# Vectors loaded as rows and turned by TensorE, an output product begun one channel early, a softmax maximum in one reduction

## The reference, cut to what matters

```python
# attention, projection (context 256 tokens, then 1024 tokens)
h = rms_norm(x, norm_w) * (1 + scale) + shift        # shift, scale, norm_w: vectors of 1024
q_a, k_a, v_a, c_q, c_kv, k_pe, gate = split(h @ w_in)
q_a = rms_norm(q_a, q_norm_w); k_a = rms_norm(k_a, k_norm_w)    # per head of 64
c_q, c_kv = rms_norm(c_q, cq_w), rms_norm(c_kv, ckv_w)
# attention, 16 heads, 1280 keys
p = softmax(q @ k.T * scale); o = p @ v
# hyena, projection: a convolution of 3 taps with a bias per channel, 3072 channels
u = sum(pad(h @ w_in)[:, j:j + L] * conv_w[j] for j in range(3)) + conv_b
# even mixer, projection: a causal convolution of 31 taps over 512 channels, with a bias
u = causal_dwconv(a_val * sigmoid(a_gate), dw_w, dw_b)
# recurrence: h_t = a_t h_(t-1) + b_t over the tokens, for 1024 channels, then
y = (gelu(y_branch) * h) @ out_w
```

## Time and profile before

| | |
|---|---|
| median of 3 runs | 5271.82 us (5264.84 to 5273.2) |
| profiled execution, its own time | 5277.84 us |
| its span | 5276.1 us |
| PE busy | 4409.4 us, 84% of the span |
| DVE, ACT, GpSimd busy | 1938.4 us, 1097.2 us, 276.5 us |

### The profile page before, as it was taken

The page is one execution under the profiler, slowest core; times in us unless marked ns, Lnnn a source line. Parts: engine busy times, 40 slices in busy tenths (PEclk is TensorE's granted clock), DMA queues, the critical chain, the costliest instruction groups (busy, mean ns, idle before and its releaser), DMA issues. The chain is left out here.

```text
span 5276.1 us, 52830 instructions
## 1 busy us (share of the span) xinstructions
PE 4409.4 (84%) x18126; PEld 2298.7 (44%) x18126; DVE 1938.4 (37%) x3064; ACT 1097.2 (21%) x1726; POOL 276.5 (5%) x390
## 2 busy tenths in 40 slices
PE   2599688997699988999689977869998598879995
PEld 0355455554344435777344445443332243533332
DVE  1233455443212205988439465321111333321112
ACT  0122344442111102222020344000000243100001
POOL 0000000000000000111000000000001000000001
PEclk7799899998899998999899988879999699789998
DMA  6322221113444411111330112356644420366655
GB/s 240 109 63 66 57 48 35 34 34 120 146 170 178 172 43 64 50 50 49 128 116 32 47 70 80 129 243 261 245 170 151 144 72 24 117 244 235 269 186 199
DMA packets 284026, 644.83 MB, mean 122 GB/s; under 512 B 92357, under 2 KB 172117, under 8 KB 264449
## 3 DMA queue, kind: packets, MB, share of 16 engines
q1 hardware_dynamic: 247594, 514.27, 28.2%
q0 software_dynamic: 21856, 102.40, 5.0%
q10 hardware_dynamic: 14456, 26.58, 1.3%
HBM read 915.53 MB, written 117.73 MB: 196 GB/s over the span
## 5 line engine op out<-in xcount | busy, mean ns | idle before, releaser
L3325 PE MATMUL blocks_h<-moe_w,blocks_xT 128*64 128x512 f32 x3072 | 694.0, 605 | 21.4 <-issue 15.3
L3325 PEld LDWEIGHTS blocks_h<-moe_w,blocks_xT 128*64 128x64 f32 x3072 | 223.6, 139 | 447.6 <-issue 442.6
L1630 PE MATMUL hyp_acc<-hy_hT,hyp_weights 128*128 128x512 f32 x768 | 337.7, 599 | 40.2 <-DMA hyp_weights<-in_hy_w_in 40.2
L3346 PE MATMUL blocks_acc<-moe_w,blocks_hidT 128*64 128x512 f32 x1536 | 340.1, 595 | 1.6 <-DVE blocks_hidT L3238 1.6
L1069 PE MATMUL att_scores<-att_kT,att_qT 64*128 64x512 f32 (+3 forms) x768 | 251.3, 546 | 21.2 <-DMA att_v<-scratch_V 21.2
L799 PE MATMUL lat_acc<-lat_w_in,lat_hT 128*128 128x512 f32 (+1 forms) x640 | 244.8, 538 | 1.5 <-DVE lat_hT L683 1.5
L1630 PEld LDWEIGHTS hyp_acc<-hy_hT,hyp_weights 128*128 128x128 f32 x768 | 146.3, 193 | 217.0 <-issue 217.0
L1093 PE MATMUL att_turn<-ident,att_probs 128*128 128x128 f32 x1280 | 192.2, 281 | 56.3 <-ACT att_probsT L981 32.1
L2166 PE MATMUL evp_acc<-ev_hT,evp_weights 128*128 128x512 f32 x512 | 225.5, 602 | 7.6 <-DVE evp_qkT L2307 5.6
L1004 DVE TENSOR_REDUCE att_parts<-att_scores 128x1 f32<-128x1024 f32 (+1 forms) x256 | 198.7, 818 | 73.5 <-PE att_scores L1069 73.5
L970 ACT ACTIVATE att_probs<-att_scores,att_nmax 128x1280 f32<-128x1280 f32 x128 | 170.0, 1328 | 193.5 <-DVE att_nmax L1006 193.5
(11 more groups left out here) (476 smaller groups left out, 5910.4 us busy)
## 6 DMA issues: line engine op xcount, KB each, us to landing
moe_w<-in_ex_w SPq DMA_DIRECT2D x288, 2048.0 KB
hyp_m_weights<-in_mod_w POOLq DMA_DIRECT2D x6, 8192.0 KB, 24.1
mod_weights<-in_ada_w SPq DMA_DIRECT2D x6, 4096.0 KB, 23.2
scratch_y_rows<-blocks_y ACTq DMA_DIRECT2D x48, 512.0 KB, 8.3
hyp_weights<-in_hy_w_in SPq DMA_DIRECT2D x8, 2048.0 KB, 27.4
scratch_parts<-hyp_uT SPq DMA_DIRECT2D x24, 512.0 KB, 3.5
evp_weights<-in_ev_in_w SPq DMA_DIRECT2D x5, 2048.0 KB, 12.7
lat_w_in<-in_attn_w_in SPq DMA_DIRECT2D x4, 2048.0 KB, 18.0
```

What stands on the lines that cost most here:

```text
L1630: mm = nc.tensor.matmul(acc[:, m % 2, half * NC:(half + 1) * NC], weights[:, ws, kt, c:c + P], hT[:, kt, half * NC:(half + 1) * NC], start ...
L3325: mm = nc.tensor.matmul(out[mine, :], xT[:, s, kt, mine], w[:, l, kt, :], start=(kt == 0), stop=(kt == KT - 1))
L3346: mm = nc.tensor.matmul(acc[mine, c, :], hidT[:, kt, mine], w2[:, l, kt, c * NC:(c + 1) * NC], start=(kt == 0), stop=(kt == FT - 1))
```

## The change

Five places change.

1. In the attention projection (both runs) the three vectors are loaded as 24 rows of 128 into `col_rows` and turned by one PE transpose; DVE copies them to `cols`. SP loads x of tile 0, the rows, the first chunk of `w_in`, x of tile 1, then the rest. The four loads of head norm weights move from SP's to ScalarE's queue, under a semaphore of their own, and DVE waits for them after the first tile's `hT`. ACT squares before it waits for `gain`.
2. In attention one reduction over 1280 columns takes the place of two reductions and the minimum.
3. In the hyena projection taps and bias are loaded as 96 rows of 128, turned by one PE transpose and copied by DVE.
4. In the even projection the tap rows come first in SP's queue; the bias moves behind the second weights, with a semaphore that DVE alone waits for.
5. In the recurrence the first two token tiles use px and py, and their products over channel tiles 0 to 6 begin when tile 6 is scanned; the last matmul of each follows when tile 7 is.

```diff
@@ attention_project, SP
-                for s in range(S):
-                    load_x(0, s)
+                load_x(0, 0)
                 for n, v in enumerate((d["mods"][vec, 0:D], d["mods"][vec, D:2 * D], d["norm_w"][0])):
-                    sp.dma_start(cols[:, n, :], columns(v), allow_slow_non_contiguous=True).then_inc(cols_in, 16)
-                for dst, v, count in ((w_head[:, 0:GQ, :], "attn_q_norm", GQ), (w_head[:, GQ:, :], "attn_k_norm", GKV)):
...
-                sp.dma_start(w_low[:, 0:MQR], row(d["mla_q_norm"][0], P)).then_inc(cols_in, 16)
-                sp.dma_start(w_low[:, MQR:], row(d["mla_kv_norm"][0], P)).then_inc(cols_in, 16)
+                    sp.dma_start(col_rows[n * KT:(n + 1) * KT, :], v.rearrange("(kt p) -> kt p", p=P)).then_inc(cols_in, 16)
                 for c, (a, b) in enumerate(chunks):
                     sp.dma_start(w_in[:, :, a:b], wv[:, :, a:b]).then_inc(w_chunk_in[c], 16)
+                    if c == 0:
+                        load_x(0, 1)
@@ ACT
-                act.wait_ge(prepared, signals(1))
+                for dst, v, count in ((w_head[:, 0:GQ, :], "attn_q_norm", GQ), (w_head[:, GQ:, :], "attn_k_norm", GKV)):
+                    act.dma_start(dst, row(d[v][0], P).unsqueeze(1).to_broadcast([P, count, HD])).then_inc(heads_in, 16)
+                act.dma_start(w_low[:, 0:MQR], row(d["mla_q_norm"][0], P)).then_inc(heads_in, 16)
+                act.dma_start(w_low[:, MQR:], row(d["mla_kv_norm"][0], P)).then_inc(heads_in, 16)
...
                 def prepare(n, s):
                     square(n, s)
+                    act.wait_ge(prepared, signals(1))
                     modulate(n, s)
@@ DVE
-                dve.wait_ge(cols_in, signals(16 * 7))
...
+                def columns_ready():
+                    dve.wait_ge(cols_turned, signals(1))
+                    nc.vector.tensor_copy(cols[:, :, :].rearrange("p v kt -> p (v kt)"), up[:, 0, 0:3 * KT]).then_inc(cols_ready, 1)
+                    dve.wait_ge(cols_ready, signals(1))
...
+                def head_weights_ready():
+                    dve.wait_ge(heads_in, signals(16 * 4))
...
                 def prepare(n, s):
+                    columns_ready()
                     norm(n, s)
                     modulate(n, s)
+                    head_weights_ready()
@@ PE
+                pe.wait_ge(cols_in, signals(16 * 3))
+                nc.tensor.transpose(up[:, 0, 0:3 * KT], col_rows[:, :], ident[0:3 * KT, 0:3 * KT]).then_inc(cols_turned, 1)
                 pe.sem_inc(copied, 2)
@@ stage_attention, DVE maximum
-                    b = j % 2
-                    for i, (ready, a, z) in enumerate(((front_scored, 0, 2 * NC), (scored, 2 * NC, KEYS))):
-                        dve.wait_ge(ready, signals(n * PAIR + (j + 1)))
-                        nc.vector.tensor_reduce(parts[:, b, i:i + 1], scores[:, b, a:z], AX.X, ALU.max, negate=True).then_inc(halved, 1)
-                    dve.wait_ge(halved, signals(n * (2 * PAIR) + (2 * j + 2)))
-                    nc.vector.tensor_tensor(nmax[:, b:b + 1], parts[:, b, 0:1], parts[:, b, 1:2], ALU.min).then_inc(maxed, 1)
+                    dve.wait_ge(scored, signals(n * PAIR + (j + 1)))
+                    nc.vector.tensor_reduce(nmax[:, j % 2:j % 2 + 1], scores[:, j % 2, 0:KEYS], AX.X, ALU.max,
+                                            negate=True).then_inc(maxed, 1)
@@ stage_hyena_project
-                for j in range(TAPS):
-                    sp.dma_start(taps[:, j, :], columns(d["hy_conv_w"][0, j]), allow_slow_non_contiguous=True)\
-                        .then_inc(taps_in, 16)
-                sp.dma_start(bias[:, :], columns(d["hy_conv_b"][0]), allow_slow_non_contiguous=True).then_inc(taps_in, 16)
+                sp.dma_start(tap_rows[0:TAPS * COLS, :], d["hy_conv_w"][0].rearrange("j (q p) -> (j q) p", p=P)).then_inc(taps_in, 16)
+                sp.dma_start(tap_rows[TAPS * COLS:, :], d["hy_conv_b"].rearrange("a (q p) -> (a q) p", p=P)).then_inc(taps_in, 16)
@@ PE, ahead of pe.sem_inc(product, CH_TILES)
+                pe.wait_ge(taps_in, signals(32))
+                rows = (TAPS + 1) * COLS
+                nc.tensor.transpose(turn[:, 0, 0, 0:rows], tap_rows[:, :], ident[0:rows, 0:rows]).then_inc(taps_turned, 1)
@@ stage_even_project, SP
+                sp.dma_start(tap_rows[:, :], d["ev_dw_w_2"][0]).then_inc(taps_in, 16)
                 load(1, 1)
-                sp.dma_start(tap_rows[:, :], d["ev_dw_w_2"][0]).then_inc(taps_in, 16)
-                sp.dma_start(bias[:, :], columns(d["ev_dw_b_2"][0]), allow_slow_non_contiguous=True).then_inc(taps_in, 16)
                 load(0, 0)
+                sp.dma_start(bias[:, :], columns(d["ev_dw_b_2"][0]), allow_slow_non_contiguous=True).then_inc(bias_in, 16)
@@ PE
-                pe.wait_ge(taps_in, signals(32))
+                pe.wait_ge(taps_in, signals(16))
@@ stage_recurrence, PE
+                pe.wait_ge(scanned, signals(KT - 1))
+                pe.wait_ge(conved, signals(KT))
+                pe.wait_ge(gelued, signals(KT))
+                for t in range(2):
+                    for c in range(2):
+                        output(t, c, range(KT - 1))
                 pe.wait_ge(scanned, signals(KT))
...
+                for t in range(2):
                     for c in range(2):
...
+                        output(t, c, [KT - 1]).then_inc(product, 1)
+                for t in range(2, TT):
+                    for c in range(2):
+                        pe.wait_ge(scaled, signals(2 * t + c - 3))
+                        output(t, c, range(KT)).then_inc(product, 1)
```

More of the change, by code:

```diff
@@ L1475, in stage_hyena_project @@
         weights = sb("weights", [P, 2, KT, NC])
-        taps, bias = sb("taps", [P, TAPS, HY_PARTS * CH_TILES]), sb("bias", [P, HY_PARTS * CH_TILES])
+        COLS = HY_PARTS * CH_TILES
+        tap_rows, taps = sb("tap_rows", [(TAPS + 1) * COLS, P]), sb("taps", [P, TAPS + 1, COLS])
         u = sb("u", [P, 2, L])
@@ L1487, in stage_hyena_project @@
         w_in = [sem(f"w_in{s}") for s in range(2)]
[L1488 to L1489 removed]
+        taps_in, taps_turned, taps_ready, product, centred, sides, conved, turned, uT_act, uT_dve = (
+            sem(n) for n in ("taps_in", "taps_turned", "taps_ready", "product", "centred", "sides", "conved", "turned", "uT_act", "uT_dve"))
         part_out = [sem(f"part_out{s}") for s in range(2)]
@@ L1564, in centre @@
                     act.wait_ge(turned, signals(q * 2))
-                    nc.scalar.activation(u[:, s, :], acc[:, s, :], ACT.Identity, bias=bias[:, bass.ds(q, 1)],
+                    nc.scalar.activation(u[:, s, :], acc[:, s, :], ACT.Identity, bias=taps[:, TAPS, bass.ds(q, 1)],
                                          scale=taps[:, 1, bass.ds(q, 1)]).then_inc(centred, 1)
```

48 lines of the change are left out of this document (25 added, 23 removed).

## The result

The changed kernel takes **5225.6 us** (median of 4 runs, 5223.0 to 5229.7) against 5270.5 (4 runs of the kernel before beside it): ratio 0.9917, 95% interval 0.9900 to 0.9934. Forecast were 5200.7 us and a range of 5184 to 5225. The profiled execution has a span of 5224.6 us against 5276.1. The sign was right, the size was not: 71.1 us were forecast, 51.5 came between the spans and 45 between the medians. The profiled execution of the kernel before was itself 7.4 us slower than its median, the one of the changed kernel 0.8, so some 6 us of what the two traces differ by need not be the change's.

What follows compares the result with a forecast made beforehand. PE, busy 84% of the span, was taken to lose time in idle stretches waiting for loads and other engines. Gains 36 + 13 + 8.4 + 2 + 11.7 = 71.1 us gave 5200.7 us, range 5184 to 5225.

Steps and rivals of the forecast that it cites:

- Part 1: Attention projection, `ctx` and `lat`: earlier first products gain 18 us each, 36 in all, ends 32.9 and 43.9.
- If they alternate one for one and the repeated reads keep their own pace of 83 per us: Attention projection: `w_in`'s first chunk beside head weights takes 13.8 us, product starts at 108, gain 16.3 us in `ctx`.
- the turned columns hide in it: Attention projection: transposing and copying 24 row pieces fits within the 6.64 us from ACT's square to first product.
- Rival (a): Attention projection: head weights still hold SP's queue up; two stages give 12 us, not 36; 5224.7 us; chance 0.17.
- Rival (b): Attention projection: the queues do not hinder each other at all; 43.9 us instead of 36; 5192.8 us; chance 0.20.
- Part 2: Attention's softmax maximum: one reduction shortens 57 waits by 0.24 us each; gain 13 us, ends 0 and 18.
- (c): Attention gains nothing because the later maximum takes the wait's place; 13 us less, 5213.7 us; chance 0.10.
- (d): Attention slower: exponent due once each tile is scored, longer tail loses 117 us; 5331 us; chance 0.03.
- Part 3: Hyena projection: 96 pieces of 512 B replace 12,288 of 4 bytes; gain 8.4 us, ends 6.5 and 14.
- Part 4: Even projection: transposes stop waiting for the bias, gate weights then decide; gain 2 us, ends 1 and 3.2.
- Rival (e): Hyena and even projections gain nothing, weights still waiting for other traffic; 10.4 us less, 5211 us; chance 0.06.
- Part 5: Recurrence's end: output products start after tile 6 is scanned; gain 11.7 us, ends 10.5 and 12.5.

Runs made afterwards that it cites:

- 8 heads after x: Changed kernel, but ScalarE issues the repeated head weights only once x has landed, some 4 us later; 5219.8 us (0.9892).
- 5 columns on ScalarE: Changed kernel with the three column-row loads moved from SP's to ScalarE's queue, ahead of the head weights; 5209.0 us (0.9880).
- 6 one load ahead: Changed kernel with two of three column-row loads on ScalarE's queue, only the norm weight's rows left ahead of `w_in`; 5218.1 us (0.9900).
- 7 w_in first: Changed kernel with the three column-row loads put behind `w_in`'s first chunk in SP's queue; 5236.9 us (0.9932).
- 6 columns merged: Changed kernel with shift and scale rows in one load instead of two; 5225.7 us (0.9912).
- Experiment 9: Changed kernel with the repeated head weights issued on GpSimd's queue in place of ScalarE's; 5226.5 us (0.9915).
- experiment 3: Changed kernel with the same head weight pieces read from an address of their own per partition, so norms get wrong weights; 5201.2 us (0.9869).
- experiment 4: Changed kernel with ScalarE's four head weight loads issued only after `w_in`'s first chunk landed and its half of `hT` was written; 5211.8 us (0.9895).

## Why the prediction was wrong, point by point

**Part 1 failed, at one step:** "If they alternate one for one and the repeated reads keep their own pace of 83 per us". The pace of the reads was near enough (78 alone, 58 beside `w_in`), and they can alternate one for one, as the earlier trace rows had it (466 beside 464, 344 beside 332). But in the changed kernel they don't alternate: SP's queue gets 34 packets beside 1093 in 14 us, and `w_in`'s packets start only near 113, when few of the head weights are left. The first product stands at 27.2 us in place of the 16.2 that this step gives at its one-for-one end. Two queues alternated from the start only where `w_in`'s issue was clearly first. The runs with the head weights on ScalarE's queue, by the lead of `w_in`'s issue over that of the head weights in `ctx`, against the first product there:

```
experiment            w_in ahead by   first product
8 heads after x          2.06 us          15.2
5 columns on ScalarE     0.75             15.25
6 one load ahead        -0.18             20.0   (lat: -0.14, 26.4)
7 w_in first            -0.47             31.7   (columns behind w_in)
6 columns merged        -1.30             27.1
the changed kernel      -1.50             27.2
```

The change issues its head weights 1.5 us before `w_in`, since ScalarE has nothing else to do at the start, while SP has x and three row loads first. Experiment 9 stands outside this table: there `w_in` was 0.8 us ahead of GpSimd's loads, and the product still came at 27.1. I took the share from stretches in which both queues were already full; they do not say who gets in. That it is set off by the repeated reads, experiment 3 shows. Why ScalarE's queue keeps SP's out, and not only slows it, and what ends that before the repeated reads are through (experiment 7), no run shows. The step "the turned columns hide in it" failed by the same cause: turned at 111.86, not near 98; experiment 7 shows that the small loads are its victims and not its source.

Rival (a) is what happened, 12 us for the two starts where 5.3 + 5.1 = 10.4 came, and 5224.7 in all. That this total is within 1 us of the measured one is in part luck: Part 1 gave 3.9 us more than its 12, most of it by the clock, and the last step below took about as much back. The rival had a chance of 0.17, too little: its ground, that the pace comes from the reads and not from the queue, was in the earlier trace rows and is what experiment 3 shows. Rival (b) fails by the changed kernel's own trace. The rule of the Trainium skill (DMA: Bandwidth & Descriptors, section "Issuing engines are not separate DMA queues") is that loads issued on several engines share the same DMA engines and interleave. The sharing held, the interleaving did not: 34 packets beside 1093. So the 33 us that I took from it were too much as well.

The wait for the head weights is covered, as forecast: they were ready at 117.2, later than the 111.3 forecast, and the next norm was due at 132. Where `w_in` got in early the cover is gone: 11.2 us of PE in experiment 4.

**Part 2** came as worked out, in size and in place: 0.25 us less in each of 56 waits is 14 us; stage 12.7, undone 14.7. Rivals (c) and (d) fall: no new wait for the exponent took the gain. **Part 3** gave 9.2 against 8.4, and the closeness is in part luck. The rows were turned 2.0 us after their issue, not 3, but the first product gained 7.5 and not 8.4, since the weights landed a microsecond later than worked out. The other 1.7 came behind the first product, where the code is the same; over the 15 traces with the new code the stage takes 569.5 to 573.1 us. **Part 4** gave 0.7 against 2: the first product comes 10.1 us after the stage's first load in place of 11.5, and the tap rows took 4.9 us to be turned. The stage takes 335.1 to 337.7 us in the traces with the new code and took 337.65 before, so a gain of 2 is neither shown nor excluded, and no run undoes this part alone. Rival (e) falls for Part 3. **Part 5** gave 12.6 against 11.7; the last matmuls of the first four halves followed without a wait, and DVE was in time.

With Part 1 at its measured 15.9 the sum is 51.0, and the profiled execution comes to 5277.84 - 51.0 = 5226.8; it took 5226.4. That agrees better than it should, since 4.8 of the 15.9 go with the clock. The last step, from there to the median, failed too, by 5 us: I took off 6.0, as before, but the changed kernel's median lies only 0.8 below its profiled execution.

## What to carry to other kernels

Don't let a transfer repeat a short row to all partitions, least of all several times each: bring it once and copy it out on the chip, for some 30 us here. Where such a load must stay, issue it after the large load that the stage waits for, on a hardware queue: the best such run was 17 us faster than the changed kernel (experiment 5), and part of what it gains at the start is lost behind it. On another engine's queue it is not out of the way, on GpSimd's not even when issued later (experiment 9). And when a share between queues is read from a trace, look whether it shows how the sharing begins.

## What the hardware showed that I had not expected

- Pieces of 256 B that read one row: 78 per us (20 GB/s) over all 16 engines; the same pieces from addresses of their own: 992 in a microsecond.
- While they run on ScalarE's queue, SP's, issued 0.5 us later, moves nothing for 9 us, with a recorded engine share of 7%, and comes in before they are through (experiment 7); issued 0.75 us earlier it gets packet for packet (experiment 5).
- In GpSimd's queue the same loads hold an engine 2.2 us per 3.2 KB packet and leave SP's queue 8 packets per us.
- TensorE's clock, after the same pause of 3.5 us, stayed at its upper level in 5 of 14 traces and fell to the lower one in 9, with up to 5 us between them; traces of the same `ctx` code are among both.
